# Mixer of a two-layer trunk: four more gate projections as fp32r products, their low parts by VectorE

## The reference

```python
h = adaln(rmsnorm(x))                      # 264 x 1024
proj = h @ w_in                            # one combined projection:
# S5 input 512, q/k/v 1536, output gate 512, decay and beta, gate A 1024, gate B 1024
a = glu(gelu(s5(u)))                       # branch A, S5 state space model, then GLU
b = gated_delta(q, k, v, decay, beta)      # branch B, delta rule (GDN)
mix = sigmoid(gate_a) * a + sigmoid(gate_b) * (b @ w_b)
x = x + adaln_gate * (mix @ w_out)
```

## Time and profile before

| | us |
|---|---|
| median of 3 runs | 1902.88 |
| lowest and highest | 1896.71, 1906.61 |
| profiled execution, its own time | 1899.62 |
| its span in the profile | 1897.6 |
| TensorE busy | 1848.0 (97%) |
| VectorE busy | 734.8 (39%) |
| ScalarE busy | 446.0 (24%) |
| GpSimd busy | 242.0 (13%) |

### The profile page before, as it was taken

How to read it: one execution, slowest core, us unless ns; L and a number is a source line. 1 busy time by engine, 2 the same in 40 slices (tenths; PEclk the granted TensorE clock), 3 DMA queues, 4 the chain that set the end, 5 groups by cost and what they waited for, 6 DMA issues and landing times.

```text
span 1897.6 us, 55426 instructions
## 1 busy us (share of the span) xinstructions
PE 1848.0 (97%) x24862; PEld 1376.8 (73%) x24862; DVE 734.8 (39%) x1579; ACT 446.0 (24%) x843; POOL 242.0 (13%) x281
## 2 busy tenths in 40 slices
PE   7999999999999999999899999999999999999997
PEld 3778898899999777898866666666666666666664
DVE  6896548655575696538600100101101011100112
ACT  2214334545433224334310000001010000000101
POOL 2641423000001541333100000000000000000000
PEclk9999998999999899998999999999999999999999
DMA  9477444555554366344489999999989999999992
GB/s 357 176 273 256 153 154 157 199 183 183 178 171 129 106 209 222 134 167 167 159 340 383 394 383 395 381 382 391 389 316 382 383 392 385 389 378 395 378 395 112
DMA packets 143140, 525.45 MB, mean 277 GB/s; under 512 B 16192, under 2 KB 16704, under 8 KB 142272
## 3 DMA queue, kind: packets, MB, share of 16 engines
q1 hardware_dynamic: 140544, 508.82, 72.0%
q10 hardware_dynamic: 1728, 7.85, 1.2%
q0 software_dynamic: 640, 5.35, 0.8%
HBM read 515.52 MB, written 6.43 MB: 275 GB/s over the span
## 4 chain that ended last, share of the span: by engine, by line
PE 92%; DVE 4%; ACT 1%; issue 1%; DMA 1%; ACTq 0%; SPq 0%; DVEq 0%
PE bank L1054 46%; PE bank L910 13%; PE bank L297 10%; PE bank L650 8%; PE bank L514 4%; PE bank L530 2%; PE bank L1062 1%; PE bank L479 1%; PE bank L995 1%; DMA masks<-in_masks 1%; PE bank L456 1%; PE bank L894 1%; PE bank L724 0%; DMA ring<-in_w 0%; PE bank L1003 0%
## 5 line engine op out<-in xcount | busy, mean ns | idle before, releaser
L1054 PE MATMUL bank<-ring,arena 128*32 128x256 f32 x16128 | 877.3, 379 | 0.0
L1054 PEld LDWEIGHTS bank<-ring,arena 128*32 128x32 f32 x16128 | 520.5, 110 | 344.8 <-issue 2.3
L297 PE MATMUL bank<-hT,ring 128*128 128x264 f32 x864 | 207.8, 401 | 5.0 <-issue 3.0
L2432 DVE TENSOR_TENSOR arena<-arena,bank 128x128 f32<-128x128 f32 x168 | 38.3, 283 | 424.0 <-ACT arena L1560 424.0
L297 PEld LDWEIGHTS bank<-hT,ring 128*128 128x128 f32 x864 | 168.3, 197 | 41.8 <-issue 11.9
L1560 ACT ACTIVATE arena<-bank 128x128 f32<-128x128 f32 x168 | 34.4, 277 | 448.7 <-PE bank L1054 448.7
L910 PE MATMUL bank<-hh,whi 128*128 128x264 f32 x448 | 128.0, 286 | 2.1 <-DVE hl L2462 1.5
L910 PE MATMUL bank<-hh,wlo 128*128 128x264 f32 x448 | 126.9, 283 | 0.0
L910 PE MATMUL bank<-hl,whi 128*128 128x264 f32 x448 | 126.8, 283 | 0.0
L2454 DVE TENSOR_TENSOR wlo<-ring,whi 128x1024 fp32r<-128x1024 f32 x84 | 102.3, 1224 | 61.3 <-ACT whi L1450 61.2
L2341 DVE COPY arena<-bank 32x256 f32<-32x256 f32 x24 | 10.2, 427 | 291.6 <-PE bank L1054 291.3
(11 more groups left out here) (421 smaller groups left out, 2485.6 us busy)
## 6 DMA issues: line engine op xcount, KB each, us to landing
ring<-in_w SPq DMA_DIRECT2D x964, 512.0 KB, 5.9
out_gdns<-arena POOLq DMA_DIRECT2D x2, 2048.0 KB, 8.3
arena<-in_gdn ACTq DMA_DIRECT2D x2, 1536.0 KB, 7.2
xT<-in_x ACTq DMA_DIRECT2D x1, 1056.0 KB, 9.0
out_y<-hT SPq DMA_DIRECT2D x4, 264.0 KB, 2.1
arena<-in_gdn ACTq DMA_DIRECT2D x2, 512.0 KB, 4.5
masks<-in_masks ACTq DMA_DIRECT2D x1, 512.0 KB, 11.1
cpk<-in_cpk SPq DMA_DIRECT2D x1, 512.0 KB, 5.3
```

The costliest lines, as they stand in the source:

```text
L297: ins = pe.matmul(out, w, rhs, start=start, stop=stop)
L1054: ins = pe.matmul(o[32 * j:32 * j + 32, 0:DQ], x(t), w[:, DQ * c:DQ * c + DQ], start=first, stop=last)
L2432: ins = v.tensor_tensor(erow[:, c % 3, r, :], srow[:, c % 2, r, :], up_bank(c, r)[:, P:2 * P], ALU.mult)
```

## The change

Seven gates in plain fp32 become three (`WHOLE = 3`, the y gates). Norm, k, ln and e (`GATE_VEC = 4`) become fp32r products. Their low parts are made by VectorE (`gate_low`, a new function, counted in `ulo_done`) at three places of its list; those of the nine later gates stay with GpSimd. ScalarE's `gate_high` now stands three gates ahead and not two: parts 0 and 1 behind the last gelu, part 2 before the exps of the decay, part 3 behind the sigmoid of the norm gate, and so on. The copy `mg` moves from behind the k gate to the place behind the Square of L1324, ahead of the gelus, and `lg` on GpSimd from behind the second `e_done` to behind the third y gate, ahead of two small output transfers. The buffers of the three pairs are rotated, since the pair in the arena is now the first.

```diff
-WHOLE = sum(UNITS[s] for s in ("y", "norm", "k", "ln", "e"))
+WHOLE, GATE_VEC = UNITS["y"], sum(UNITS[s] for s in ("norm", "k", "ln", "e"))
...
 # TensorE, unit(u)
-                        pe.wait_ge(sem("vlo_done"), GATE_S * l + i + 1)
+                        if i < GATE_VEC:
+                            pe.wait_ge(sem("ulo_done"), (GATE_VEC + GLU_S) * l + i + 1)
+                        else:
+                            pe.wait_ge(sem("vlo_done"), (GATE_S - GATE_VEC) * l + i - GATE_VEC + 1)
...
 # ScalarE, unit(l, u)
-                    if WHOLE <= u < 2 * KD - 2:
-                        gate_high(l, u - WHOLE + 2)
+                    if WHOLE <= u < 2 * KD - 3:
+                        gate_high(l, u - WHOLE + 3)
...
                 act.activation(sq, cv[:, 0:2 * NH, :], ACT.Square).then_inc(sem("qk_sq"), 1)
+                act.activation(mg[:, :, :], hT[:, :, :], ACT.Copy).then_inc(sem("high_in"), 1)
...
+                gate_high(l, 0)
+                gate_high(l, 1)
                 act.wait_ge(sem("nrm_ss"), l + 1)
...
+                gate_high(l, 2)
                 for c in range(NC):
                     name = ("gcb", l, c)
...
-                for step in ("norm", "k"):
+                for step in ("norm", "k", "ln", "e"):
                     fill(step)
-                act.activation(mg[:, :, :], hT[:, :, :], ACT.Copy).then_inc(sem("high_in"), 1)
-                fill("ln")
-                gate_high(l, 0)
-                gate_high(l, 1)
-                fill("e")
...
 # VectorE, gdn
                 v.wait_ge(sem("cv_silu"), 3 * (l + 1))
+                gate_low(l, 0)
                 qk_sums(l)
                 name = ("gcc", l)
                 gc = gd[:, 5, 0:8]
                 takes(v, v.tensor_copy(gc, filled(v, name)[:, 0:8]), name)
+                gate_low(l, 1)
...
+                    if c == 0:
+                        gate_low(l, 2)
+                        gate_low(l, 3)
                     name = ("kk", l, c)
...
+            def gate_low(l, i):
+                v.wait_ge(sem("uhi_done"), (GATE_S + GLU_S) * l + i + 1)
+                hi, lo = usplit[i % len(usplit)]
+                v.tensor_tensor(lo[:, :], ring[:, unit_at(l, WHOLE + i) % RING, :], hi[:, :].bitcast(F32),
+                                ALU.subtract).then_inc(sem("ulo_done"), 1)
...
 # GpSimd
+                filled(pool, ("in", l, UT + S5_STEPS + WHOLE - 1))
+                pool.wait_ge(sem("high_in"), 2 * l + 1)
+                pool.tensor_tensor(lg[:, :, :], hT[:, :, :], mg[:, :, :].bitcast(F32), ALU.subtract).then_inc(sem("low_in"), 1)
                 pool.wait_ge(sem("cvo_done"), l + 1)
                 pool.dma_start(conv_out[l], cvo[:, :, :, :]).then_inc(sem("parts_out"), 16)
                 pool.wait_ge(sem("s5o_done"), l + 1)
                 pool.dma_start(s5_out[l], s5o[:, :, :, :]).then_inc(sem("parts_out"), 16)
-                filled(pool, ("in", l, UT + S5_STEPS + WHOLE - 1))
                 pool.wait_ge(sem("e_done"), NC * (l + 1))
-                pool.wait_ge(sem("high_in"), 2 * l + 1)
-                pool.tensor_tensor(lg[:, :, :], hT[:, :, :], mg[:, :, :].bitcast(F32), ALU.subtract).then_inc(sem("low_in"), 1)
-                for i in range(GATE_S):
-                    if i == 2:
+                for i in range(GATE_VEC, GATE_S):
+                    if i == GATE_VEC + 2:
```

More of the change, by code:

```diff
@@ L214, in trunk_program @@
         mg, lg = over("mg", [P, KD, N], slab_at, NH * (3 + N) + 4), over("lg", [P, KD, N], where(hT), 0)
-        upairs = ((where(bpk), 0, where(ckk), 0), (where(cpk), 0, where(bt), 0), (arena_at, 12 * B1, arena_at, 13 * B1))
+        upairs = ((arena_at, 12 * B1, arena_at, 13 * B1), (where(bpk), 0, where(ckk), 0), (where(cpk), 0, where(bt), 0))
         usplit = [(over(f"uhi{i}", [P, SLOT * P], a, b), over(f"ulo{i}", [P, SLOT * P], c, e))
@@ L616, in unit @@
                             pe.wait_ge(sem("low_in"), 2 * l + 2)
-                        pe.wait_ge(sem("ulo_done"), GLU_S * l + m + 1)
+                        pe.wait_ge(sem("ulo_done"), (GATE_VEC + GLU_S) * l + GATE_VEC + m + 1)
                         for half in range(2):
```

## The result

The changed kernel takes 1928.28 us (median of 5 runs, 1926.37 to 1931.70) against 1901.90 (5 runs, 1896.08 to 1906.61) for the kernel before: ratio 1.0158, 95% interval 1.0138 to 1.0179. These two medians are 26.4 us apart and alone give 1.0139; the five runs of the kernel before are spread over 10.5 us, and in the 13 to 29 runs beside the experiments its median was 1897.4 to 1898.5, against which 1928.28 is 1.0157 to 1.0163. Its profiled execution took 1928.60, with a span of 1926.7 and a mean granted clock of 0.983.

A forecast was written before the change was run, and what follows sets the result against it. TensorE was taken as the bound, with VectorE close (0.8 us of reserve). Per layer 6.3 + 3.9 + 2 x 1.7 = 13.6, 26.5 for both, gave 1926.1 on the profiled execution, 1929.4 on the median; forecast 1928 us, range 1909 to 1943.

The forecast's parts named there:

- Step 1: Norm and k gates: the moved copy on ScalarE makes decay columns 2.5 us late, the k gate's end 1.75.
- same spacing: Layer 1's steps were taken to be spaced as layer 0's, lacking only 0.7 us of small operations.
- the 0.3 that was left outside the sum: GpSimd's `lg` could hold VectorE's small S5 operations, starting low part 0 near 169.0: some 0.3 us per layer.
- Step 2: The e gate's low part on VectorE waits for slot 84; mask 7.1 us later, 6.3 us per layer behind the second `e`.
- the 6.3: Delay in us per layer behind the second `e`, taken to contain the norm and k gates' delay too.
- Step 3: Three gates ahead: ScalarE waits for slot 95 ahead of copying `yl`, so TensorE waits 3.9 us per layer.
- The clock: Half-clock stretches behind TensorE's stalls at the norms and at `yl`: 1.7 us each, between 0 and 3.4.
- swallowed: TensorE's stall of about 3 us near 190: its clock loss disappears in a following wait for VectorE.
- The gain: fp32r gates 0.64 us shorter each on TensorE, 8 in two layers, 5.1 us at most; lost for ln and e.

The follow-up runs named there:

- e4: Changed kernel with ScalarE's high parts of the norm and k gates right behind the input copy, ahead of the gelus: 1927.62 us, ratio 1.0153.
- e9: Changed kernel with the e gate's low part later on VectorE, two gates ahead on ScalarE, and norm and k gate work reordered: 1902.16 us, ratio 1.0021.
- e1: Changed kernel with the e gate's low part moved on VectorE behind the small sample operations: 1919.49 us, ratio 1.0112.
- e6b: Changed kernel with 11 and 12 matmuls that compute nothing in TensorE's two stalls per layer: 1921.03 us, ratio 1.0127.
- e7: e9 with the e gate's low part on GpSimd and not on VectorE: 1903.64 us, ratio 1.0027.

## Why the prediction was right or wrong

- **Step 1: right in kind, too small.** The columns came 1.9 late (2.5 forecast), TensorE waited 2.53 for the norms (2.85), the k gate ended at 180.2 (180.7). But these places met the forecast with TensorE 2.3 us ahead at the y gates' end; counted from there the k gate's end came 3.6 later in layer 0 and 5.5 in layer 1, not 1.75. ScalarE's row had no such lead: its Square began 0.3 earlier than before. And layer 1 lacks the "same spacing" of the sum: before, the last gelu ended 2.6 us behind the y gates in layer 0 (165.73 and 163.1), 5.3 in layer 1 (740.34 and 735.07).
- **`lg`: hidden as forecast, as long as ScalarE holds.** In the changed kernel low part 0 waits for ScalarE in both layers, so the 0.3 that was left outside the sum was nothing. In layer 0 of e4, with the copies early, VectorE was held beside `lg` instead: the held operation ended at 168.16, `lg` at 168.13. The rule from the Trainium skill, page "GPSIMD Engine Reference", § 1 Specifications, agrees with this row: a start of low part 0 near 169.0 by the rule, 169.17 measured. In e9, with the rest mended, the rows make the hold the larger part of a 1.9 us delay; no run without it shows that.
- **Step 2: the cause right, the last stretch of the path not.** Slot 84 was issued at 181.9 (182.45 forecast), landed 4.42 later (4.3), the mask came at 188.6 (189.1), the second `e` at 208.1 (208.4). e1 shows the cause, not only the place: with low part 3 elsewhere 4.4 us per layer go. But TensorE didn't wait for the second `e`. Its squarings began at 206.74, 6.5 late, and after two products of 1.84 us it asked for this `e` at 208.6, 0.5 behind its end. What made it late was the stall of 3.65 us on the scaled q, which the forecast took to lie inside the 6.3, and the half clock behind it. In e6b, with that stretch at full clock, TensorE does wait 1.30 for VectorE.
- **Step 3: the mechanism right, one place of it missed.** The wait for slot 95 moved the x products' end from 8.7 to 15.1 behind, 6.4, where 3.9 and 1.7 of clock were forecast. Missed was the same lookahead behind the e gate's sigmoid: ScalarE was held for slot 91 until 210.86, ahead of the squarings' copies, so that the pr2 gate began at 223.70, 8.7 behind and not 6.3. The order of ScalarE's list showed that row too; I followed only the turn gate's.
- **The clock: the places wrong, the sum near.** Forecast were 1.7 behind the first and the third stall, and nothing behind the one near 190, "swallowed" by VectorE. In layer 0 the first had none, the other two 6.80 us each; in layer 1 all three had one. The one near 190 was not swallowed: the ln and e gates behind it lie on the chain to slot 91. e6b gives some 3 us per layer for the second and third, with the wide interval named there, against 3.4 forecast for the first and third; that the two are close is luck.
- **The gain: as forecast, it shows nowhere.** No run isolates it. By the order, norm, ln and e stand ahead of waits of TensorE, and only the k gate's 0.64 could count.
- **The total** of 1928 met 1928.28, but by errors that cancel in part. The mixers lost some 36 us in the profiled pair, not 27: the missed wait for slot 91, a step 1 of 3.6 and 5.5, and the clock. About 7 came back outside them, most of it where the kernel before had longer half-clock stretches in that execution. The sum gave 1926.1 on the profiled execution and 1929.4 on the median of three runs, and 1928 between them was chosen without a reason; the 3.3 us between these two are not in the later runs of the kernel before, whose medians lie 1.1 to 2.2 below that execution. The runs of one kernel spread over 5 to 10 us, and a forecast from one execution can be no better than that.

Left open: why the stretches at half clock are 3.4, 6.8 or 10.3 us behind stalls that look alike, and whether they make the spread of the runs; and whether `lg` in a buffer of its own, made before the y gates end, would close the last 4 us of e9. No run has it; it would need 8.4 KB more per partition (8 x 264 x 4 bytes).

## What to carry to other kernels

Before an operation that needs a streamed slot is put into an engine's list, ask when that slot can be issued at the earliest, here six slots ahead of TensorE, and what stands behind the operation on that engine: the wait by itself can cost little, the queue behind it is what costs. In e1 ScalarE still waits 7.99 us for slot 84, and 4.4 us per layer are gone, since VectorE's mask no longer stands behind it. Do it for every row that a longer lookahead adds, not for the one that comes to mind. And count a faster instruction as a gain only where its engine isn't about to wait for another one: of 5.1 us saved on TensorE's gates here, by the order of the lists at most 1.3 could count.

## What was not expected of the hardware

- A VectorE operation of 16 elements took 2.71 to 3.87 us beside one GpSimd subtraction of 4.7 us (4.63 in layer 1 of e9); it ended with GpSimd's instruction (748.25 + 3.87 = 752.1, as 747.40 + 4.69). It was not only operations with two inputs: a copy of 32 elements with one input took 2.14 beside 2.35 of GpSimd (e7). The Trainium skill, page "GPSIMD Engine Reference", § 1 Specifications, names VectorE's instructions in a 2-port mode beside those with two inputs; whether this copy is one, no run here shows.
- Filling two stalls of TensorE per layer with matmuls that compute nothing took the ratio from 1.0158 to 1.0127, though no wait was taken away; the difference is at the edge of what the runs can tell.
